# Retention stage of a hybrid decoder layer: bias rows loaded between the token tiles, masked sample values on ScalarE, state products ahead of the samples' output

## The chip, the cores and the metric

The kernel runs on one core of a Trainium2 chip. The metric is the device time of one execution in microseconds (us); less is better. Engine names: PE is TensorE (matmuls and transposes), DVE is VectorE, ACT is ScalarE, POOL is GpSimd, SP is SyncE, which here only issues DMAs. L12 is line 12 of the kernel before.

## The reference, cut to what matters

One decoder layer runs on a prompt (1024 tokens) and on samples (8 sequences of 8 new tokens, so 64 rows). The input projection makes `z`, whose columns are queries, keys, values and gate of the retention and queries, keys, values of the attention. Retention is computed per head (8 heads of width 64) in chunks:

```
inner = einsum('bihd,bjhd->bhij', q, k) * decay
o     = einsum('bhij,bjhe->bihe', inner, v) + einsum('bihd,bhde->bihe', q, S) * cross_decay
S_new = S * exp(C * log_g) + einsum('bjhd,bjhe,jh->bhde', k, v, k_decay)
o     = group_norm(o) * g_ret * silu(gate)
```

The samples bring a state of their own for each sequence (8 x 8 heads x 64 x 64), so their output needs `q @ S` with the old state, and their new state needs `k^T v` within each sequence. The attention, which comes after, adds a bias that depends on the distance of key and query (`rel_bias[t5_bucket(dist)]`); the table of it for the samples, `bias_s`, is built within the retention stage.

## The kernel before, in words

The kernel is a row of stages with a barrier after each: input projection, retention (`retention`, L638), prompt attention, sample attention, output projection and FFN. Only the retention stage is touched. Each engine has its own instruction list there, written out by hand, and the engines meet only through semaphores. The tokens are tiles t = 0 to 7 of 128 prompt rows and tile 8, `SAMPLE`, of 64 sample rows.

**SP (L691 to L715).** In this order: the loads of `zr` tiles 2 to 8 out of scratch memory (L698, issued at L185; tiles 0 and 1 were loaded by the stage before); `tables.load` (L589), which issues `rel_bias` three times into `rel` (L592), the small table `whose` (L593), and the large `dist_s` (L594); after POOL's clearing the state `S_in` (L702); the stores of mix tiles 0 and 1 (`store`, L695); eight loads of the prompt's bias, `bias_p` (L598); the stores of mix tiles 2 to 7; loads for the next stage (L965); the prompt's last state (L712); the store of the samples' mix; a wait until `bias_p` has landed.

**PE (L876 to L957).** For each tile `inner(t+1)` (L896: scores of keys and queries), `output(t)` (L913 and L916), `turn(t+2)` (L885: transposes of q and k), `update(t+1)` (L904: the state). `inner(t)` waits for `inT_ready` t, which DVE's `scores(t-1)` raises. After the loop: the first part of the samples' distance table (`sample_products`, L632, part 0); the samples' output (L938 with the old state, L941 with the inner scores), signalled by `o_done`; the samples' state products (L950), which write the four PSUM banks `su_ps`, `in_ps` (two) and the second of `o_ps`, with one signal for each of the four head pairs; parts 1 and 2 of the table (L632); and, after the samples' output is centred, filler matmuls (`keep_awake`, L146).

**DVE (L770 to L874).** For each tile t: `scores(t)` (L779), `centre(t-1)` (L812, L814, L818), `carry(t+1)` (L799), at t = 2 also `tables.build_rows` (L615: the six products rel times whose), `variance(t-1)` (L824, L826), `finish(t-2)` (L833). `build_rows` waits until all of `rel` and `whose` have landed (`landed` 64). `finish(t)` writes the mix tile into one of two buffers `mixr`, so for t >= 2 it waits until the store of tile t-2 has landed (L832). After the loop: the sample scores, the sample queries (L788), `centre(7)`, `last_state` (L799, L807), `variance(7)`, `finish(6)`, then `one_sequence` for sequences 0 to 4 (L685), `finish(7)`, part 0 of the table out of PSUM (L622), `centre(SAMPLE)`, and four `decode_state` (L866: new state of a head pair) with `variance(SAMPLE)` after the first and `finish(SAMPLE)` after the third.

`vm` holds, for each sequence, the sample values with all other sequences' rows set to zero; `bmask[:, b]` is 1 for the rows of sequence b. DVE makes five of them and POOL three:

```
eng.tensor_tensor(vm[:, b, :], head(SAMPLE, 2, 0, NH).unsqueeze(1).broadcast_to(shape),
                  spread(bmask[:, b], shape), ALU.mult).then_inc(vm_ready, 1)
```

**ACT (L743 to L768).** For each tile `evacuate(t+2)` (L750, L751: q and k out of PSUM) and `square(t)` (L758); at the end `square(SAMPLE)` and parts 1 and 2 of the table (L622).

**POOL (L717 to L741).** For each tile `late(t)` (L728: the power -0.5 of the variance; L730: the product with it), at t = 3 the decayed keys `kd` (L737), at t = 5 its share of `vm` (L685), and at the end `late(SAMPLE)`.

Of the kernel before, what the change touches and what calls it, by code (L numbers as in the profile page):

```python
# [27 lines left out]
ALU = mybir.AluOpType  # L28
# [5 lines left out]
WID = NH * HD  # L34
# [114 lines left out]
def spread(ap, shape):  # L149

    return ap.unsqueeze(2).broadcast_to(shape)
# [9 lines left out]
class RetentionInputs:  # L161
# [21 lines left out]
    def load(self, eng, z, t):  # L183
        n = tile_rows(t)
        eng.dma_start(self.zr[t][0:n].rearrange("p a h d -> p (a h d)"), z[t * 128:t * 128 + n, 0:4 * WID]).then_inc(self.landed[t], 16)  # L185
# [383 lines left out]
class DistanceTables:  # L569
# [16 lines left out]
         self.bias_landed) = map(  # L586
            sem, ("landed", "samples_landed", "ones_set", "rel_t_ready", "bias_done", "bias_ready", "bias_landed"))

    def load(self, sp):  # L589
        sp.wait_ge(self.ones_set, 1)  # L590
        for n in range(3):
            sp.dma_start(self.rel[n * self.K:n * self.K + N_BUCKETS, :], self.A["rel_bias"]).then_inc(self.landed, 16)  # L592
        sp.dma_start(self.whose[:, :], self.A["c_whose"]).then_inc(self.landed, 16)  # L593
        sp.dma_start(self.dist_s[:, :, :], self.A["c_dist_s"]).then_inc(self.samples_landed, 16)  # L594

    def load_bias(self, eng):
# [41 lines left out]
def retention(nc, A, z, mix, ident, ret, state_p, tab, bias_p, bias_s, kept_on, stored, sout_ready, ahead):  # L638


    with ExitStack() as ctx:
# [33 lines left out]
        def head(t, a, h, n=1):  # L675
            return zr[t][0:tile_rows(t), a, h:h + n, :].rearrange("t h d -> t (h d)")

        def by_sequence(p, r):
            return sample_ps[p][HD * r:HD * r + HD].rearrange("d a c -> d (a c)").rearrange("d (b e) -> d b e", e=HD)

        def one_sequence(eng, b):

            shape = [NS, b.stop - b.start, WID]
            eng.wait_ge(landed[SAMPLE], 16)
            eng.tensor_tensor(vm[:, b, :], head(SAMPLE, 2, 0, NH).unsqueeze(1).broadcast_to(shape),  # L685
                              spread(bmask[:, b], shape), ALU.mult).then_inc(vm_ready, 1)

        with nc.Block() as block:

            @block.sync  # L690
            def _(sp):  # L691
                def store(t):
                    rows = tile_rows(t)
                    sp.wait_ge(mix_ready, t + 1)
                    sp.dma_start(mix[t * 128:t * 128 + rows, :], mixr[0:rows, t % 2, :]).then_inc(mix_stored[t % 2], 16)  # L695

                for t in range(2, TT):
                    ret.load(sp, z, t)  # L698
                tables.load(sp)
                sp.wait_ge(cleared, 4)  # L700
                for par in range(2):
                    sp.dma_start(S_in[HD * par:HD * par + HD, :, :, HD * par:HD * par + HD],  # L702
                                 A["state_ret"][0].rearrange("b (p r) d e -> r d b p e", r=2)[par]).then_inc(state_landed, 16)
                store(0)
                store(1)
                tables.load_bias(sp)
                for t in range(2, PT):
                    store(t)
                ahead(sp)
                sp.wait_ge(last_ready, 2)  # L710
                for par in range(2):
                    sp.dma_start(state_p.rearrange("(p r) d e -> r d p e", r=2)[par],  # L712
                                 S_last[HD * par:HD * par + HD]).then_inc(state_stored, 16)
                store(SAMPLE)
                tables.finish(sp)  # L715

            @block.gpsimd  # L717
            def _(pool):
                pool.memset(mhalf[:, :], -0.5).then_inc(cleared, 1)
                pool.memset(S[:, :, :, :], 0.0).then_inc(cleared, 1)  # L720
                pool.memset(qdm[:, :, :], 0.0).then_inc(cleared, 1)
                pool.memset(S_in[:, :, :, :], 0.0).then_inc(cleared, 1)
                pool.wait_ge(cleared, 1)

                def late(t):
                    rows = tile_rows(t)
                    pool.wait_ge(var_ready, t + 1)
                    pool.tensor_tensor(stat[0:rows, t, 4, :], stat[0:rows, t, 3, :], mhalf[0:rows, :], ALU.pow).then_inc(rstd_ready, 1)  # L728
                    pool.wait_ge(rstd_ready, t + 1)
                    pool.tensor_tensor(oc[0:rows, t % 2], oc[0:rows, t % 2], spread(stat[0:rows, t, 4, :], [rows, NH, HD]),  # L730
                                       ALU.mult).then_inc(on_ready, 1)

                for t in range(PT):
                    late(t)
                    if t == 3:
                        pool.wait_ge(landed[SAMPLE], 16)
                        pool.tensor_tensor(kd[:, :, :], zr[SAMPLE][0:NS, 1], spread(last_s[:, :], [NS, NH, HD]),  # L737
                                           ALU.mult).then_inc(kd_ready, 1)
                    if t == 5:
                        one_sequence(pool, slice(DEC_B // 2 + 1, DEC_B))  # L740
                late(SAMPLE)  # L741

            @block.scalar  # L743
            def _(act):
                def evacuate(t):
                    rows = tile_rows(t)
                    act.wait_ge(qk_turned, t + 1)
                    if t >= 2:
                        act.wait_ge(o_done, t - 1)
                    act.copy(qT[:, t % 2, :, 0:rows], qk_ps[0][:, :, 0:rows])  # L750
                    act.copy(kT[:, t % 2, :, 0:rows], qk_ps[1][:, :, 0:rows]).then_inc(qkT_ready, 1)  # L751

                def square(t):
                    rows = tile_rows(t)
                    act.wait_ge(oc_ready, t + 1)
                    if t:
                        act.wait_ge(square_sum_ready, t)
                    act.activation(sq[0:rows], oc[0:rows, t % 2], ACT.Square).then_inc(sq_ready, 1)  # L758

                evacuate(0)  # L760
                evacuate(1)
                for t in range(PT):
                    if t + 2 < TT:
                        evacuate(t + 2)
                    square(t)
                square(SAMPLE)
                for n in (1, 2):
                    tables.build_samples(act, act.copy, n, table_ps[n])  # L768

            @block.vector  # L770
            def _(dve):
# [37 lines left out]
                def centre(t):  # L809
                    rows = tile_rows(t)  # L810
                    dve.wait_ge(o_done, t + 1)
                    dve.tensor_reduce(stat[0:rows, t, 0, :], o_ps[t % 2][0:rows], AXX, ALU.add).then_inc(sum_ready, 1)  # L812
                    dve.wait_ge(sum_ready, t + 1)
                    dve.tensor_scalar(stat[0:rows, t, 1, :], stat[0:rows, t, 0, :], -1.0 / HD, None, ALU.mult).then_inc(mean_ready, 1)  # L814
                    dve.wait_ge(mean_ready, t + 1)
                    if t >= 2:
                        dve.wait_ge(mix_ready, t - 1)
                    dve.tensor_tensor(oc[0:rows, t % 2], o_ps[t % 2][0:rows], spread(stat[0:rows, t, 1, :], [rows, NH, HD]),  # L818
                                      ALU.add).then_inc(oc_ready, 1)
# [33 lines left out]
                last_state()  # L853
                variance(PT - 1)
                finish(PT - 2)
                one_sequence(dve, slice(0, DEC_B // 2 + 1))
                finish(PT - 1)
                tables.build_samples(dve, dve.tensor_copy, 0, table_ps[0])
                centre(SAMPLE)
                dve.wait_ge(state_landed, 32)  # L860

                def decode_state(p):
# [4 lines left out]
                                                 chunk_s[rows, p:p + 1], by_sequence(p, r), ALU.mult, ALU.add).then_inc(sout_ready, 1)  # L867

                decode_state(0)
                variance(SAMPLE)  # L870
                decode_state(1)
                decode_state(2)
                finish(SAMPLE)
                decode_state(3)  # L874

            @block.tensor  # L876
            def _(pe):
# [46 lines left out]
                for t in range(PT):  # L924
# [4 lines left out]
                    if t + 1 < PT:  # L929
                        update(t + 1)  # L930
                tables.sample_products(pe, 0, table_ps[0])
                pe.wait_ge(state_landed, 32)
                pe.wait_ge(qd_ready, 1)
                pe.wait_ge(inT_ready, SAMPLE + 1)
                pe.wait_ge(oc_ready, SAMPLE - 1)
                for p in range(NPAIR):
                    for b in range(DEC_B):
                        pe.matmul(o_ps[0][0:NS, 2 * p:2 * p + 2, :].rearrange("t h d -> t (h d)"),  # L938
# [2 lines left out]
                        mm = pe.matmul(o_ps[0][0:NS, 2 * p + r, :], inT[0:NS, r, p, 0:NS], head(SAMPLE, 2, 2 * p + r),  # L941
                                       start=False, stop=(r == 1))
                mm.then_inc(o_done, 1)
                pe.wait_ge(kd_ready, 1)
                pe.wait_ge(vm_ready, 2)
                pe.wait_ge(last_ready, 2)
                pe.wait_ge(oc_ready, PT)
                for p in range(NPAIR):
                    for r in range(2):
                        mm = pe.matmul(by_sequence(p, r), kd[:, 2 * p + r, :], vm[:, :, HD * (2 * p + r):HD * (2 * p + r + 1)],  # L950
                                       start=True, stop=True)
                    mm.then_inc(update_done, 1)
                pe.wait_ge(qkT_ready, TT)
                for n in (1, 2):
                    tables.sample_products(pe, n, table_ps[n])
# [2021 lines left out]
```

## Time and profile before

| what | us |
|---|---|
| runs of the kernel before (3) | 1560.14 to 1569.92, median 1566.24 |
| profiled execution: time | 1573.37 |
| profiled execution: span | 1571.6 |
| retention stage within the span, first PE instruction to last | 366.06 to 448.43 |
| PE busy over the span | 1489.1 (95%) |
| DVE, ACT, POOL busy | 809.4 (52%), 557.0 (35%), 310.4 (20%) |
| mean granted clock of PE | 0.988 of full speed |

The span is the time from the first to the last record of the profiled execution; the device time has 1.8 us more around it. The profiled execution is 7.1 us longer than the median of the runs. All times in the rows below are us from the start of the span. In a timeline row the first number is the start and the second the time from there to the end of the last of its instructions.

### The profile page before, as it was taken

The numbers are of one execution on the slowest core, as the hardware profiler recorded it, in microseconds if no ns is written. First come the engines' busy times: TensorE is split into PE (matmuls) and PEld (weight loads), VectorE is DVE, ScalarE is ACT, GpSimd is POOL, SyncE is SP. The second block draws the span as 40 slices with busy tenths as digits, with TensorE's granted clock in tenths as the row PEclk, the third lists the DMA queues.
The fourth block names the chain that finished last, engine by engine and source line by source line (L and its number), as shares of the span: only waits on it lengthen the run. The fifth ranks groups of instructions, "written<-read, shape, count | busy, mean of one in ns | idle before, by whom it ended". The sixth has DMA issues, their size and how long they took to land.

```text
span 1571.6 us, 23194 instructions
## 1 busy us (share of the span) xinstructions
PE 1489.1 (95%) x8974; PEld 1279.6 (81%) x8974; DVE 809.4 (52%) x1396; ACT 557.0 (35%) x1054; POOL 310.4 (20%) x362
## 2 busy tenths in 40 slices
PE   7999999998988888898999999999999999999987
PEld 6788888887855556776889999999999999888766
DVE  2333211103766654443456966766676675755455
ACT  4401112212134543443333433343333333545442
POOL 3246420002532323100464010000001000000001
PEclk9999999999899999999999999999999999999999
DMA  5346554527565724993366587989898985877865
GB/s 207 99 134 193 174 188 146 184 97 252 180 222 149 206 78 194 420 408 106 126 197 191 182 210 220 213 225 227 208 237 167 244 194 174 290 241 225 245 232 203
DMA packets 138830, 317.77 MB, mean 202 GB/s; under 512 B 23948, under 2 KB 65180, under 8 KB 133573
## 3 DMA queue, kind: packets, MB, share of 16 engines
q1 hardware_dynamic: 129928, 229.26, 44.0%
q0 software_dynamic: 6976, 71.32, 20.9%
q10 hardware_dynamic: 1824, 15.83, 2.4%
q8 instruction: 65, 1.06, 0.3%
q14 instruction: 37, 0.30, 0.1%
HBM read 254.45 MB, written 137.92 MB: 250 GB/s over the span
## 4 chain that ended last, share of the span: by engine, by line
PE 40%; POOL 3%; DMA 3%; DVE 3%; issue 3%; ACT 1%; SPq 1%; DVEq 0%; POOLq 0%; ACTq 0%
PE y_ps L2760 28%; PE y_ps L2844 4%; PE y_ps L2750 3%; PE x_ps L2844 3%; DMA raw_step<-wt_scratch 2%; POOL xm L1712 1%; POOL h_lo L1726 1%; DVE slot_lo L2447 1%; PE y_ps L1845 1%; DVE y L1810 1%; PE m_ps L2771 1%; PE d_ps L2771 1%; PE m_ps L2844 0%; PE d_ps L2844 0%; SPq L2122 0%
## 5 line engine op out<-in xcount | busy, mean ns | idle before, releaser
L518 PE MATMUL z_ps<-w_hi,h_hi 128*128 128x512 f32 x488 | 191.4, 392 | 4.3 <-POOL h_lo L335 4.3
L518 PE MATMUL z_ps<-w_lo,h_hi 128*128 128x512 f32 x488 | 190.7, 391 | 0.0
L2760 PE MATMUL y_ps<-h_hi,slot_lo 128*128 128x320 f32 (+1 forms) x560 | 179.8, 321 | 0.0
L2760 PE MATMUL y_ps<-h_hi,slot_hi 128*128 128x320 f32 (+1 forms) x560 | 179.8, 321 | 0.0
L2760 PE MATMUL y_ps<-h_lo,slot_hi 128*128 128x320 f32 (+1 forms) x560 | 179.5, 321 | 0.0
L518 PE MATMUL z_ps<-w_hi,h_lo 128*128 128x512 f32 x432 | 168.7, 391 | 0.0
L131 POOL DMA_DIRECT2D ks_sample<-cache_k_win x60 | 34.1, 568 | 630.9 <-PE y_ps L2760 389.4
L2447 DVE TENSOR_TENSOR slot_lo<-raw_step,slot_hi 128x512 fp32r<-128x512 f32 x132 | 85.2, 687 | 85.9 <-ACT slot_hi L2257 85.8
L518 PEld LDWEIGHTS z_ps<-w_hi,h_hi 128*128 128x128 f32 x488 | 91.9, 188 | 24.6 <-POOL h_lo L335 4.9
L2257 ACT CAST slot_hi<-raw_step 128x512 fp32r<-128x512 f32 x132 | 75.3, 618 | 95.0 <-DMA raw_step<-wt_scratch 39.7
L2760 PE MATMUL y_ps<-s_hi,slot_hi 128*128 128x384 f32 x320 | 107.7, 337 | 0.0
L2760 PE MATMUL y_ps<-s_hi,slot_lo 128*128 128x384 f32 x320 | 107.7, 336 | 0.0
L2760 PE MATMUL y_ps<-s_lo,slot_hi 128*128 128x384 f32 x320 | 107.5, 336 | 0.0
L518 PEld LDWEIGHTS z_ps<-w_lo,h_hi 128*128 128x128 f32 x488 | 92.1, 189 | 18.9
L2760 PEld LDWEIGHTS y_ps<-h_hi,slot_lo 128*128 128x128 f32 x560 | 105.2, 188 | 0.0
L2760 PEld LDWEIGHTS y_ps<-h_lo,slot_hi 128*128 128x128 f32 x560 | 105.2, 188 | 0.0
L2760 PEld LDWEIGHTS y_ps<-h_hi,slot_hi 128*128 128x128 f32 x560 | 105.2, 188 | 0.0
L430 DVE TENSOR_TENSOR w_lo<-w_raw,w_hi 128x2048 fp32r<-128x2048 f32 x14 | 32.0, 2288 | 124.1 <-ACT w_hi L365 124.1
L518 PEld LDWEIGHTS z_ps<-w_hi,h_lo 128*128 128x128 f32 x432 | 81.5, 189 | 17.1
L2447 DVE TENSOR_TENSOR slot_lo<-raw,slot_hi 128x512 fp32r<-128x512 f32 x104 | 69.9, 691 | 30.1 <-ACT slot_hi L2257 28.8
L2299 ACT COPY held<-y_ps 128x384 f32<-128x384 f32 x60 | 28.7, 479 | 118.1 <-PE y_ps L2760 118.1
L2257 ACT CAST slot_hi<-raw 128x512 fp32r<-128x512 f32 x104 | 62.2, 619 | 11.3 <-PE y_ps L2760 8.7
(369 smaller groups left out, 3200.7 us busy)
## 6 DMA issues: line engine op xcount, KB each, us to landing
ks_sample<-cache_k_win POOLq DMA_DIRECT2D x60, 544.0 KB, 8.5
vs_sample<-cache_v_win POOLq DMA_DIRECT2D x60, 544.0 KB, 10.9
raw<-w_gu SPq DMA_DIRECT2D x20, 1024.0 KB, 15.4
raw_step<-f_scratch SPq DMA_DIRECT2D x66, 256.0 KB, 3.9
K<-cache_k_win SPq DMA_DIRECT2D x8, 2048.0 KB
w_raw<-w_in SPq DMA_DIRECT2D x14, 1024.0 KB
z_scratch<-z_out SPq DMA_DIRECT2D x56, 256.0 KB, 2.3
raw_d<-w_down SPq DMA_DIRECT2D x11, 1024.0 KB, 12.3
```

Of the source, the lines that this page charges most:

```text
L131: eng.dma_start(flat(new)[:, bass.ds(row * WID, n * WID)], flat(old)[:, bass.ds(row * WID + DEC_T * WID, n * WID)]).then_inc(kept, 16)
L430: dve.tensor_tensor(w_lo[cut], w_raw[:, q], w_hi[cut].bitcast(F32), ALU.subtract).then_inc(w_lo_ready, 1)
L518: mm = pe.matmul(z_ps[t % 3][:, :], x[:, k, t * 128:t * 128 + 128], w[:, par, k, :], start=(k, n) == first, stop=(k, n) == last)
L1712: pool.tensor_tensor(self.xm[:, t % 2, :], self.y[:, :], self.inputs.x_n[:, t % 2, :], ALU.add).then_inc(self.xm_ready, 1)
L1726: pool.tensor_tensor(self.h.lo[at][cut], self.hg[:, q, :, 0:n], self.h.hi[at][cut].bitcast(F32), ALU.subtract).then_inc(self.lo_ready, 1)
L2257: act.copy(in_slot(slot_hi, n), source(n)).then_inc(hi_ready, 1)
L2299: act.copy(held[:, k, :], chain_a[:, 0:384]).then_inc(held_ready, 1)
L2447: dve.tensor_tensor(in_slot(slot_lo, n), source(n), in_slot(slot_hi, n).bitcast(F32), ALU.subtract).then_inc(lo_ready, 1)
L2750: mm = pe.matmul(bank[u % 2][:, 0:n], w, x, start=(k, m) == (0, 0), stop=(k, m) == (KT - 1, 2))
L2760: mm = pe.matmul(bank[:, 0:cols], w, v[:, k, :], start=fresh and (k, m) == (0, 0), stop=(k, m) == (HK - 1, 2), skip_group_check=True)
L2771: mm = pe.matmul(sample_ps[c], f_s[:, sub, :], w[n % RING][:, :], start=(g, sub, e) == (0, 0, 0), stop=(g, sub, e) == (LAST, 1, 1), skip_g ...
L2844: mm = pe.matmul(bank, x[:, own], w[:, :], start=fresh and m == 0, stop=ends and m == 2, skip_group_check=True)
```

## The change

Four edits, all in the retention stage.

1. `tables.load` is split. The three loads of `rel` and the one of `whose` are issued after the `zr` loads of tiles 2 and 3; `dist_s` keeps its place behind all seven.
2. DVE's five masked sample values go to ACT, as five copies with a scale of one column of `bmask`: two after `square(6)`, three after `square(7)`. POOL keeps its three. `vm_ready` thus reaches 6 instead of 2.
3. Part 0 of the table goes out of PSUM on ACT, after those three copies, in place of DVE.
4. PE issues the samples' state products before the samples' output. DVE does all four `decode_state` first, then `centre`, `variance` and `finish` of the samples.

```diff
-    def load(self, sp):
+    def load_rows(self, sp):
         sp.wait_ge(self.ones_set, 1)
         for n in range(3):
             sp.dma_start(self.rel[...], self.A["rel_bias"]).then_inc(self.landed, 16)
         sp.dma_start(self.whose[:, :], self.A["c_whose"]).then_inc(self.landed, 16)
+
+    def load_distances(self, sp):
         sp.dma_start(self.dist_s[:, :, :], self.A["c_dist_s"]).then_inc(self.samples_landed, 16)
...
+        ON_ACT = DEC_B // 2 + 1
...
                 for t in range(2, TT):
                     ret.load(sp, z, t)
-                tables.load(sp)
+                    if t == 3:
+                        tables.load_rows(sp)
+                tables.load_distances(sp)
...
+                def own_values(sequences):
+                    act.wait_ge(landed[SAMPLE], 16)
+                    for b in sequences:
+                        act.activation(vm[:, b, :], head(SAMPLE, 2, 0, NH), ACT.Copy, scale=bmask[:, b:b + 1]).then_inc(vm_ready, 1)
...
                     square(t)
+                    if t == 6:
+                        own_values(range(2))
+                own_values(range(2, ON_ACT))
+                tables.build_samples(act, act.copy, 0, table_ps[0])
                 square(SAMPLE)
...
                 finish(PT - 2)
-                one_sequence(dve, slice(0, DEC_B // 2 + 1))
                 finish(PT - 1)
-                tables.build_samples(dve, dve.tensor_copy, 0, table_ps[0])
-                centre(SAMPLE)
                 dve.wait_ge(state_landed, 32)
...
                 decode_state(0)
-                variance(SAMPLE)
                 decode_state(1)
                 decode_state(2)
+                decode_state(3)
+                centre(SAMPLE)
+                variance(SAMPLE)
                 finish(SAMPLE)
-                decode_state(3)
...
                 tables.sample_products(pe, 0, table_ps[0])
+                pe.wait_ge(kd_ready, 1)
+                pe.wait_ge(vm_ready, 1 + ON_ACT)
+                pe.wait_ge(last_ready, 2)
+                pe.wait_ge(oc_ready, PT)
+                pe.wait_ge(inT_ready, SAMPLE + 1)
+                for p in range(NPAIR):
+                    for r in range(2):
+                        mm = pe.matmul(by_sequence(p, r), kd[...], vm[...], start=True, stop=True)
+                    mm.then_inc(update_done, 1)
                 pe.wait_ge(state_landed, 32)
                 pe.wait_ge(qd_ready, 1)
-                pe.wait_ge(inT_ready, SAMPLE + 1)
-                pe.wait_ge(oc_ready, SAMPLE - 1)
                 for p in range(NPAIR):
...
                 mm.then_inc(o_done, 1)
-                pe.wait_ge(kd_ready, 1)
-                pe.wait_ge(vm_ready, 2)
-                pe.wait_ge(last_ready, 2)
-                pe.wait_ge(oc_ready, PT)
-                for p in range(NPAIR):
-                    for r in range(2):
-                        mm = pe.matmul(by_sequence(p, r), kd[...], vm[...], start=True, stop=True)
-                    mm.then_inc(update_done, 1)
                 pe.wait_ge(qkT_ready, TT)
```

## Rows read from the trace of the kernel before

**Rows 1.** Waits of all engines, 362 to 450 us: total us, times, longest.

```profile
DVE rel_t L615 <- DMA whose<-c_whose: 6.9, 1, 6.9
```

**Rows 2.** Timeline of DVE in the tile loop: start, us, and idle before it in brackets.

```profile
391.29 0.63 DVE L615 TENSOR_TENSOR rel_t<-rel,whose 99x24 f32<-99x24 f32 x6 [6.86 <-DMA whose<-c_whose]
...
402.28 1.29 DVE L779 TENSOR_TENSOR inT<-in_ps,mask 128x512 f32<-128x512 f32 x2 [3.31 <-PE o_ps L916]
...
406.69 0.69 DVE L833 TENSOR_TENSOR mixr<-oc,zr 128x512 f32<-128x512 f32 x1
...
421.19 1.29 DVE L779 TENSOR_TENSOR inT<-in_ps,mask 128x512 f32<-128x512 f32 x2 [0.93 <-PE o_ps L916]
...
423.11 2.50 DVE L814 TENSOR_SCALAR stat<-stat 128x8 f32<-128x8 f32 x1
```

**Rows 3.** Timeline of PE in the tile loop.

```profile
394.78 2.08 PE L896 MATMUL in_ps<-qT,kT 64*128 64x128 f32 x16 [6.23 <-DVE inT L779]
...
405.04 1.16 PE L896 MATMUL in_ps<-qT,kT 64*128 64x128 f32 x16 [0.26 <-ACT kT L751]
...
411.07 1.16 PE L896 MATMUL in_ps<-qT,kT 64*128 64x128 f32 x16 [0.27 <-ACT kT L751]
```

**Rows 4.** Busy us of PE, PEld, DVE, ACT, POOL; PEclk; DMA share; GB/s.

```profile
396.00:400.00 4.00, 4.00 (x24) 3.78 (x22) 2.89 (x6) 0.63 (x1) 1.55 (x1) 0.50 0.70 156
```

**Rows 5.** Landing: zr tiles 2 and 3; stores 0 and 1; the eight bias_p loads.

```profile
DMA to landing us min/median/max: 5.2/6.2/7.3
...
DMA to landing us min/median/max: 3.4/4.1/4.8
...
DMA to landing us min/median/max: 4.9/7.2/9.8
```

**Rows 6.** DMA issues between 407.3 and 407.9 us: KB, us to landing (mix store 2).

```profile
mix_scratch<-mixr SPq DMA_DIRECT2D x1, 256.0 KB, 7.0
```

**Rows 7.** Timeline of SP's issues.

```profile
373.07 24.09 SPq L702 DMA_DIRECT2D S_in<-state_ret  x1
397.20 2.14 SPq L695 DMA_DIRECT2D mix_scratch<-mixr  x2
399.39 4.97 SPq L598 DMA_DIRECT2D bias_p<-tab_scratch  x8
```

**Rows 8.** Timeline of PE at the end of the stage.

```profile
429.47 1.93 PE L938 MATMUL o_ps<-S_in,qdm 128*64 128x128 f32 x16 [0.60 <-DVE qdm L788]
...
438.34 0.22 PE L941 MATMUL o_ps<-zr,inT 64*64 64x64 f32 x1
...
440.92 1.08 PE L950 MATMUL o_ps<-vm,kd 64*64 64x512 f32 x4
...
446.55 1.88 PE L146 MATMUL o_ps<-zr,ident 128*128 128x512 f32 x4
```

**Rows 9.** Timelines of ACT, DVE and POOL.

```profile
361.88 0.72 ACT L392 ACTIVATE z_out<-sums,stat 64x512 f32<-64x512 f32 x1 [0.76 <-DVE sums L436]
...
430.94 0.63 ACT L758 ACTIVATE sq<-oc 128x512 f32<-128x512 f32 x1 [3.95 <-DVE oc L818]
...
437.76 0.69 DVE L833 TENSOR_TENSOR mixr<-oc,zr 128x512 f32<-128x512 f32 x1 [0.94 <-POOL oc L730]
...
446.89 1.52 DVE L866 SCALAR_TENSOR_TENSOR S_out<-S_in,chunk_s,o_ps 64x512 f32<-64x512 f32 x2
...
443.11 1.63 POOL L728 TENSOR_TENSOR stat<-stat,mhalf 64x8 f32<-64x8 f32 x1 [5.38 <-DVE stat L826]
```

**Rows 10.** Timeline of PE: two long idles in the FFN stage.

```profile
1474.47 0.50 PE L2844 MATMUL y_ps<-slot_hi,slot_hi 128*128 128x512 f32 x1 [3.58 <-DVE slot_lo L2447]
...
1504.31 0.50 PE L2844 MATMUL x_ps<-slot_hi,slot_hi 128*128 128x512 f32 x1 [3.22 <-DVE slot_lo L2447]
```

**Rows 11.** Busy time by stretch behind these two idles; columns as in rows 4.

```profile
1475.80:1479.20 3.40, 3.40 (x10) 2.63 (x9) 3.40 (x6) 2.59 (x6) 0.00 (x0) 0.53 0.93 341
...
1504.30:1508.00 3.70, 3.04 (x12) 2.17 (x12) 3.70 (x7) 2.95 (x7) 0.00 (x0) 1.00 0.29 111
```

More of the change, by code:

```diff
@@ L679, in by_sequence @@
             return sample_ps[p][HD * r:HD * r + HD].rearrange("d a c -> d (a c)").rearrange("d (b e) -> d b e", e=HD)
[L681 to L686, printed above, removed]
+        ON_ACT = DEC_B // 2 + 1
         with nc.Block() as block:
@@ L739, in _ @@
                     if t == 5:
-                        one_sequence(pool, slice(DEC_B // 2 + 1, DEC_B))
+                        shape = [NS, DEC_B - ON_ACT, WID]
+                        pool.tensor_tensor(vm[:, ON_ACT:, :], head(SAMPLE, 2, 0, NH).unsqueeze(1).broadcast_to(shape),
+                                           spread(bmask[:, ON_ACT:], shape), ALU.mult).then_inc(vm_ready, 1)
                 late(SAMPLE)
@@ L931, in _ @@
                 tables.sample_products(pe, 0, table_ps[0])
+                pe.wait_ge(kd_ready, 1)
[5 more added lines that the diff above has]
+                    for r in range(2):
+                        mm = pe.matmul(by_sequence(p, r), kd[:, 2 * p + r, :], vm[:, :, HD * (2 * p + r):HD * (2 * p + r + 1)],
+                                       start=True, stop=True)
+                    mm.then_inc(update_done, 1)
                 pe.wait_ge(state_landed, 32)
                 pe.wait_ge(qd_ready, 1)
-                pe.wait_ge(inT_ready, SAMPLE + 1)
-                pe.wait_ge(oc_ready, SAMPLE - 1)
                 for p in range(NPAIR):
@@ L943, in _ @@
                 mm.then_inc(o_done, 1)
-                pe.wait_ge(kd_ready, 1)
-                pe.wait_ge(vm_ready, 2)
-                pe.wait_ge(last_ready, 2)
-                pe.wait_ge(oc_ready, PT)
-                for p in range(NPAIR):
-                    for r in range(2):
-                        mm = pe.matmul(by_sequence(p, r), kd[:, 2 * p + r, :], vm[:, :, HD * (2 * p + r):HD * (2 * p + r + 1)],
-                                       start=True, stop=True)
-                    mm.then_inc(update_done, 1)
                 pe.wait_ge(qkT_ready, TT)
```

## The prediction

> **What bounds the kernel now.** I read the page first: PE is busy 95% of the span, so only time that PE loses in this stage, or adds to its end, can count. The waits of the stage have one row that does not repeat with the tiles: DVE stands 6.9 us before the six small products of `build_rows` [rows 1]. The timelines show what hangs on it. DVE is free at 391.29 - 6.86 = 384.4 and starts at 391.3 [rows 2]; `scores(3)` is queued behind it, and PE idles 6.23 us for it before `inner(4)` [rows 3]. Then comes a second loss: with the granted clock at 0.50, the lower of the two levels (1.2 GHz), from just before PE restarts [rows 4], the tile that starts at 394.78 lasts 10.26 us, where the next lasts 6.03 [rows 3]. So this one wait costs 6.23 - 0.27 = 6.0 us idle and 4.2 us of slow work, 10.2 us together. At the end of the stage PE runs from the samples' output through the state products and the tables to the filler, 429.5 to 448.43, with no gap worth naming [rows 8], and DVE ends at 446.89 + 1.52 = 448.41 [rows 9]: the two are balanced there.
>
> **Edit 1, rows behind tiles 2 and 3.** Tiles 2 and 3 land 5.2 and 7.3 us after their issue at about 366.0 and 366.5, so by 374 [rows 5]. The four small loads (3 x 1.0 KB, 1.2 KB) stand right behind; even several us late they beat 384.4. No load is added, and the tiles behind move by the issue time of four small loads at most, some 2 us, while tile 5's transposes come only near 393. So the 6.9 us wait goes. Bounds: nothing (if the rows still land last) and the whole 10.2 us.
>
> What is late next is SP's queue. SP is held in the second `S_in` issue until 373.07 + 24.09 = 397.16 and only then issues store 0, at 397.20 [rows 7], landing 4.8 us later, at 402.0 (store 1 at 402.4) [rows 5]. Nothing in the change moves this. Before, `finish(2)`, which needs that store landed, came at 406.69 [rows 2] and never met it. With 10.2 us taken out its iteration would start at 392.9 (one tile pitch and the 6.0 us, 402.28 - 9.4: `scores(4)` had also stood behind the slow matmuls) and `finish(2)` would come 4.4 us later, at 397.3. It must wait until 402.0 and ends at 402.7; behind it on DVE is `scores(5)`, 402.7 to 404.0, for which PE's `inner(6)` waits. `inner(6)` starts at 404.1 instead of 411.07 [rows 3]: the gain is 7.0 us, not 10.2, and PE idles about 3.5 us.
>
> There is a second such place. Store 2 stands behind the eight loads of `bias_p`, whose issue ends at 404.36 [rows 7], the last landing at 403.9 + 9.8 = 413.7 [rows 5]; before, it was issued at 407.4 and landed 7.0 us later, 414.4 [rows 6]. It will land at the same time, since the 4 MB ahead of it do. `finish(4)` then is due at 412.6 and starts at 414.4; `scores(7)` starts at 415.1 instead of 421.19 [rows 2]: the gain is 6.1 us. Against that, L814 took 2.50 us at 423.11 [rows 2] beside POOL's share of `vm`; in the new phase they overlap by 1.6 us or so: 0.8 us back for DVE's chain. **Head: 6.9 us gained.**
>
> **Edits 2 to 4, the end, in the times of before.** ACT has no copy of this form in this stage; the nearest rows are the scaled copy of 64x512, 0.72 us [rows 9], and, from below, no time at all for what ACT's idle hides (two of the five fall before `square(7)`, 4 us of idle [rows 9]). I take 0.6 us for each of the three that count, between the pitch of back-to-back copies and 0.72. They follow `square(7)`, which ends at 430.94 + 0.63 = 431.57, so `vm` is ready at 433.4 (bounds 431.6 and 433.8). PE now waits for that before it may do anything of the samples: its product of part 0 ended 0.60 us before 429.47 [rows 8], so it idles some 4.6 us, or 3.8 after the head's unequal shifts. Behind this wait stand output, state products and both table parts.
>
> - State products 433.5 to 437.2 (before 438.3 to 442.0, 3.7 us [rows 8]).
> - Output, 429.47 to 438.56 before, 9.1 us [rows 8]: ends at 446.3.
> - PE then: tables 4.7 us (442.0 to 446.6 before) and filler 1.9 [rows 8]: 452.9.
> - Beside it the samples' norm: centre 1.6, square 0.65, variance 0.9, POOL 2.8 (L728 1.63 [rows 9] and the product), `finish` 0.7, SP's store 0.5: 7.1 us, so 453.4.
>
> The stage ends at 453.4 against 448.4: **the end costs 5.0 us.** What the edits save on DVE is true but hidden: the masked values and part 0 leave it, `finish(7)` comes no later than 437.76 [rows 9], and four `decode_state` of 1.52 us [rows 9] end by 438.5 + 6.1 = 444.6, before the output they used to stand beside. The old order had PE work on the output while `vm` was made; the new one leaves that cover unused.
>
> **The clock.** Two new idles, 3.5 and 3.8 us, can throw PE to its lower level. Of two like idles in the trace, 3.58 us was followed by a stretch at 0.53 and 3.22 us by none [rows 10, 11]; the 6.2 us one cost 4.2 us [rows 3, 4]. A stretch like 1475.8 to 1479.2 costs half its length, 1.7 us. Bounds for each place: 0 and 4.2 us. I take one short stretch at each: 1.7 at the end, and in the loop 0.8, because 0.9 us of it lies in the second store's wait. By the Trainium skill (TensorE: Matmul & The Clock Gate, What's actually happening) the throttled state is the default and activity releases it, which speaks against an order that opens idle on PE; the 3.22 us idle without a fall shows that here it is a matter of chance as well.
>
> **Sum.** -6.9 + 5.0 + 0.8 + 1.7 = +0.6 us on a profiled execution of 1573.37 us: 1574.0. That execution lay 7.1 us above the median, 1566.24, so the median after is 1566.8 us. A measurement of this kernel tells about 1% (16 us) from no change, and its own three runs span 10 us. The forecast is no measurable change.
>
> **The rivals.**
> - **A, the whole head is won.** `finish(2)` and `finish(4)` do not wait, and the clock stays up. For it: PE keeps a 6.03 us pitch wherever it is fed [rows 3]. Against it: the issue at 397.20 and its landing. It gives -(10.2 + 0.8) + 5.0 = -6.0: 1560.2 us. Chance 0.15.
> - **B, slower by the clock.** The mechanism is the half-speed stretch behind the new waits at `finish(2)` and ahead of the state products, each as long as the one of before: 4.2 at the end and 3.3 in the loop, so -6.9 + 5.0 + 7.5 = +5.6: 1571.8 us. It decides once the slow stretches cost more than the 1.9 us that the rest gains. This is what the page's rule makes of two idles. For it: that stretch has small matmuls like the ones here [rows 3]. Against: the one of 3.4 us [rows 11]. Chance 0.25.
> - **C, the rows do not land earlier.** The small loads complete only with what follows; the head is unchanged and the end costs 5.0 + 1.7: 1572.9 us. For it: `whose` landed only after all that was issued before it. Against: tiles 2 and 3 landed early [rows 5]. Chance 0.05.
>
> **How the numbers follow.** The forecast holds 0.55, with a range of its own of 1563 to 1570. Adding A, B and C and the spread of the runs, 1559 to 1573 holds 8 in 10. Only several errors in one direction pass 1%: faster 0.02, within 1% 0.95, slower 0.03.
>
> **What would show it.** L615 without an idle before it, near 384.4. `mixr` L833 of tile 2 waiting for the landing of a store, near 402, and again near 414; PE idle 3 to 4 us before `inner(6)`. At the end PE idle about 4 us before the first L950, released by ACT `vm`; L938 behind L950; the stage ending 1 to 2 us earlier than 448.4 where the clock stays up, later where it does not. Wrong would be: stores landing well before 400, `vm` ready before 431 in the times of before, or a stage end moved by over 6 us either way.

## The result, and the profile after

The kernel after takes 1575.44 us in the median of 14 runs (1568.34 to 1583.90), the kernel before, run beside it, 1565.83 us (14 runs, 1560.14 to 1569.92). The ratio is 1.0062, 95% interval 1.0045 to 1.0080: slower by 9.6 us, 0.6%. The prediction was no measurable change, 1566.8 us in a range of 1559 to 1573. So the forecast of "within 1%" held, but the time lies outside the range, and the loss is clear of the runs' noise. Of the runs used below, two of the kernel before (1583.36 and 4353.76 us) and one of j1 (4554.69 us) were slow runs and are left out of the medians.

The profiled execution of the kernel after took 1572.07 us (span 1570.2). From the stage's first PE instruction to the next stage's first it has 88.7 us (362.69 to 451.39), the kernel before 83.4 us (366.06 to 449.50). That is 5.3 us more, of the 9.6 of the medians. One chance thing is in it: the clock was at its lower level for 3.4 us at the very start of the stage of the kernel after (364.6 to 368.2), so its first state update began 5.75 us into the stage against 4.25 before, 1.5 us lost ahead of anything that was changed.

The waits of all engines of the kernel after, 362 to 450 us (total us, times, longest), no longer have the row of [rows 1]; the forecast wait for the stores stands among them:

```profile
DVE mixr L843 <- DMA mix_scratch<-mixr: 4.5, 2, 2.3
```

The timeline of DVE of the kernel after (start, us, idle before in brackets):

```profile
382.60 0.64 DVE L617 TENSOR_TENSOR rel_t<-rel,whose 99x24 f32<-99x24 f32 x6
...
397.74 1.19 DVE L843 TENSOR_TENSOR mixr<-oc,zr 128x512 f32<-128x512 f32 x1 [2.20 <-DMA mix_scratch<-mixr]
...
411.38 1.11 DVE L843 TENSOR_TENSOR mixr<-oc,zr 128x512 f32<-128x512 f32 x1 [2.27 <-DMA mix_scratch<-mixr]
...
442.71 0.68 DVE L822 TENSOR_REDUCE stat<-o_ps 64x8 f32<-64x512 f32 x1 [8.54 <-PE o_ps L957]
```

`build_rows` starts at once, where it had 6.86 us of idle before it [rows 2]; `finish(2)` and `finish(4)` wait for stores 0 and 2. At the end DVE is idle for 8.5 us until the samples' output is done, and its last `finish` ends at 449.4. The timelines say why, of PE:

```profile
400.39 1.16 PE L904 MATMUL in_ps<-qT,kT 64*128 64x128 f32 x16 [1.66 <-DVE inT L789]
...
413.96 0.68 PE L904 MATMUL in_ps<-qT,kT 64*64 64x64 f32 x16 [1.83 <-DVE inT L789]
...
418.50 5.43 PE L634 MATMUL table_ps<-dist_s,rel_t 99*128 99x512 f32 x6
424.01 1.97 PE L947 MATMUL su_ps<-vm,kd 64*64 64x512 f32 x4
425.75 3.65 PE L947 MATMUL in_ps<-vm,kd 64*64 64x512 f32 x8
429.16 1.94 PE L947 MATMUL o_ps<-vm,kd 64*64 64x512 f32 x4
431.03 3.67 PE L954 MATMUL o_ps<-S_in,qdm 128*64 128x128 f32 x16
```

and, of ACT,

```profile
421.99 1.93 ACT L764 ACTIVATE vm<-zr,bmask 64x512 f32<-64x512 f32 x3
```

The three late copies take 1.93 us, 0.64 each (forecast 0.6), and PE's first state product starts at their end, 423.9. The 4 us of idle that were forecast there are not in this profile: part 0 of the table, at half clock, ended at the same moment, 423.9, and hid the wait. Everything of PE from 416 to 436 runs slowly: part 0 of the table 5.43 us where it was 2.8 before, state products 424.0 to 431.1 (7.1 us against 3.7), output 431.0 to 442.6 (11.6 against 9.1 [rows 8]). Busy time by stretch (columns as in rows 4):

```profile
411.00:416.00 5.00, 3.17 (x38) 2.94 (x37) 4.37 (x6) 0.76 (x3) 4.09 (x2) 1.00 0.14 54
416.00:424.00 8.00, 7.93 (x20) 4.31 (x19) 6.43 (x16) 4.23 (x8) 3.07 (x2) 0.50 0.09 33
424.00:431.00 7.00, 6.99 (x16) 1.86 (x16) 4.22 (x6) 0.56 (x1) 3.06 (x2) 0.50 0.40 125
431.00:436.00 5.00, 5.00 (x26) 4.52 (x25) 3.04 (x5) 0.00 (x0) 0.00 (x0) 0.50 0.64 169
436.00:443.00 7.00, 7.00 (x59) 6.18 (x58) 0.29 (x1) 0.00 (x0) 0.00 (x0) 0.97 0.00 0
```

For 20 us PE is busy almost without a gap, at a granted clock of 0.50 (the 1.2 GHz level), from 416.0 to 436.4. It fell 2.0 us after PE had restarted from the 1.83 us idle before 413.96; that this idle caused it is the likely reading, not a shown one. The state products and the output alone lose 3.4 + 2.5 = 5.9 us.

All runs together say the same. Every run lists PE's mean granted clock; (1 - clock) x time is an estimate of what the lower level costs it. Its mean is 25.1 us over the 14 runs of the kernel after and 16.4 us over 102 runs of the kernel before that were taken beside the experiments below (no clocks are on record for the 14 of the result). The difference, 8.7 us, is nearly the whole of the loss; what is left of the time, 1550.5 and 1549.7 us, is the same within 1 us. So outside the clock the head's gain and the new wait cancel, much as the prediction had it. (The clock is listed to 0.001, which is 1.6 us in one run.)

### The profile page after: what moved, and what is told of

Same layout as the page of the kernel before. It is cut to its first block, busy times and chain, and to the rows that moved or that the text cites. A ratio compares the mean times of both kernels' runs of the same rounds, so it can differ in the third digit from the quotient of the medians.

```text
span 1570.2 us, 23197 instructions
## 1 busy us (share of the span) xinstructions
PE 1493.1 (95%) x8974; PEld 1279.9 (82%) x8974; DVE 805.4 (51%) x1394; ACT 561.0 (36%) x1060; POOL 310.0 (20%) x362
## 4 chain that ended last, share of the span: by engine, by line
PE 41%; POOL 3%; DMA 3%; DVE 3%; issue 2%; ACT 1%; SPq 0%; DVEq 0%; POOLq 0%; ACTq 0%
PE y_ps L2767 28%; PE y_ps L2851 4%; PE y_ps L2757 3%; PE x_ps L2851 3%; DMA raw_step<-wt_scratch 2%; POOL xm L1719 1%; POOL h_lo L1733 1%; PE y_ps L1852 1%; DVE slot_lo L2454 1%; DMA x_m<-x_mid_scratch 1%; DVE y L1817 1%; PE m_ps L2778 1%; PE d_ps L2778 1%; PE m_ps L2851 1%; PE d_ps L2851 1%
```

## The experiments

Medians are of runs beside the kernel before on the same chip, whose median was 1565.0 to 1566.8 us throughout; ratios are against it. The e, g, j, k and l runs were each taken on another chip, so a difference between groups is given by its ratios too where they say something else. "Stage" is the length as above, from the one profile, and "end" its part from tile 8's inner product on. "Clock" is the mean over the runs of the estimate (1 - clock) x time.

| kernel | median us | ratio (95%) | stage us | end us | clock us |
|---|---|---|---|---|---|
| before (beside e) | 1565.0 | | 83.4 | 26.8 | 15.0 |
| after | 1575.44 | 1.0062 (1.0045 to 1.0080) | 88.7 | 37.4 | 25.1 |
| e1 edit 1 alone | 1566.22 | 1.0002 (0.9985 to 1.0019) | 77.3 | 26.1 | 16.7 |
| e2 edits 2 to 4 | 1580.79 | 1.0096 (1.0074 to 1.0118) | 94.3 | 37.6 | 24.2 |
| e3 edits 1 to 3 | 1566.70 | 1.0008 (0.9991 to 1.0026) | 79.8 | 26.1 | 17.4 |
| e4 after + filler | 1570.07 | 1.0037 (1.0018 to 1.0057) | 80.8 | 31.5 | 17.4 |
| g1 e3, states cut | 1562.09 | 0.9967 (0.9942 to 0.9991) | 74.8 | 26.9 | 14.7 |
| g2 after, states cut | 1571.40 | 1.0024 (1.0010 to 1.0038) | 87.6 | 36.4 | 21.7 |
| j1 g2 + filler | 1566.45 | 1.0009 (0.9990 to 1.0027) | 80.2 | 32.2 | 14.5 |
| j2 e3, stores first | 1557.72 | 0.9949 (0.9929 to 0.9969) | 73.5 | 27.0 | 12.2 |
| j3 edit 1, stores first | 1559.10 | 0.9954 (0.9933 to 0.9976) | 73.5 | 27.0 | 13.8 |
| k3 e1 + 5 fillers in the loop | 1565.18 | 0.9995 (0.9981 to 1.0010) | 78.8 | 26.8 | 14.5 |
| l1 e1 + 3 fillers in the loop | 1566.61 | 0.9993 (0.9970 to 1.0016) | 77.9 | 26.1 | 14.9 |

The stages of e4, j1 and k3 hold a slow 3.4 us at their start, as that of the kernel after does (1.5 us of the stage's length).

**The edits apart.** e1 is the kernel before with edit 1; e2 the changed kernel without it; e3 has PE's and DVE's order of before back:

```diff
-                (state products, with their waits)
                 (output of the samples)
+                (state products, with their waits)
                 pe.wait_ge(qkT_ready, TT)
```

> The kernel before with edit 1 alone. Both theories of the loss (order: the state products wait ahead of the samples' output; clock: the new wait lets PE's clock fall and it stays low through what follows) put it in the end of the stage, which is not touched here: the head's 6.9 us less 0.8 for the clock, so 6 us below the kernel before, some 1560 us. Rival: the waits for the stores, which this edit uncovers, give it back: within 2 us of the kernel before, or above it.

> The changed kernel with edit 1 undone (edits 2 to 4 alone). Order theory: 5.0 us and at most one short slow stretch of 1.7: 5 to 7 us above the kernel before, some 1572 us. Clock theory: the slow stretch covers state products and output, 3 + 2.5 us and more: 10 to 12 us above, some 1577 us. If the end costs as much as in the changed kernel while the head loses its gain, it must lie above the changed kernel.

> The changed kernel with edit 4 undone: edits 1 to 3, but state products behind the output as before, and DVE's order as before. If the order (with or without the clock) is the loss, it is as fast as edit 1 alone or 1 us faster, some 1559 us. Rival: the copies on ACT are the loss, and it stays near the changed kernel, 1573 us or more.

e3 is the verdict on edits 2 and 3: with them and the old order the time is that of e1, to some 3 us. The loss is edit 4: e3 to the kernel after is 1566.7 to 1575.4. Edits 2 to 4 without edit 1 (e2) cost 15.0 us by the ratio. That is above even what the clock theory had (10 to 12); the expectation's 1559 us for e3 was missed as well, since it counted on e1's gain. By the estimate from the clock, 9.3 us of e2's loss against the kernel before beside it are the clock, and 5.6 us are the rest. In e2 PE idled for the masked values and all behind it ran slowly, by the timeline of PE and then the busy time by stretch (columns as in rows 4) of e2:

```profile
433.52 1.97 PE L943 MATMUL su_ps<-vm,kd 64*64 64x512 f32 x4 [4.63 <-ACT vm L760]
```

```profile
433.00:445.00 12.00, 11.47 (x38) 5.92 (x39) 7.74 (x12) 0.89 (x2) 3.06 (x2) 0.51 0.49 143
```

The idle of 4.63 us is the 4.6 us of the prediction; the slow stretch, 13.7 us long, is what was not in the sum. e1 missed: edit 1 alone gives nothing, where 6 us were forecast; its rival, that the waits for the stores give the gain back, has the time.

**The clock at the end.** e4 puts matmuls on PE ahead of the waits for the state products:

```diff
                 tables.sample_products(pe, 0, table_ps[0])
+                pe.wait_ge(oc_ready, SAMPLE - 1)
+                keep_awake(pe, o_ps[0][:, :, :], ident[:, :], head(2, 0, 0, NH), 4)
                 pe.wait_ge(kd_ready, 1)
```

> The changed kernel with four filler matmuls of 128x128 by 512 columns (1.9 us at full clock, 3.4 at the lower) on PE ahead of the wait for the masked values. Order theory: PE waits there anyway and the clock matters little, so no change against the changed kernel, 0 to +2 us. Clock theory: the filler lifts the clock or keeps it up, state products (7.0 us against 3.7) and output (11.6 against 9.1) shorten, 3 to 6 us below the changed kernel, some 1570 us.

The timeline of PE, and then the busy time by stretch, of e4:

```profile
418.12 3.60 PE L146 MATMUL o_ps<-zr,ident 128*128 128x512 f32 x8
422.22 1.08 PE L949 MATMUL su_ps<-vm,kd 64*64 64x512 f32 x4 [0.50 <-ACT vm L764]
```

```profile
418.00:436.00 18.00, 17.50 (x108) 11.33 (x107) 12.23 (x23) 2.94 (x5) 4.82 (x4) 1.00 0.37 110
```

The fillers took 3.60 us, not the 1.9 of the expectation (four fillers are eight matmuls in the trace). The time fell by 5.4 us against the kernel after (3.9 by the ratios, whose intervals overlap) although PE had more to do, and the clock's share fell from 25.1 to 17.4 us. In this profile the clock had not fallen in the loop either, so one thing was still open: whether the fall comes from the loop's waits or from the new one. g2 takes the second of the loop's two waits away and leaves 1.75 us of PE's idle at the first, j1 adds the fillers again, and g1 is g2 with the old order:

```diff
-                (S_in of all eight sequences)
+                load_states(slice(0, DEC_B // 2))
                 store(0)
                 store(1)
+                load_states(slice(DEC_B // 2, DEC_B))
+                store(2)
                 tables.load_bias(sp)
```

> Edits 1 to 3 with the order of before (as e3), and the loads of the samples' states cut in two halves: one ahead of mix stores 0 and 1, one behind them, and the bias loads behind store 2. If the waits for the stores (3.2 us in e3) and the slow stretch behind them (10.2 us long in e3) eat the head's gain, both go: the inner product of tile 8 starts near 50 us after the stage's start instead of 53.6, and the median lies 4 to 6 us below e3, some 1561 us. Rival: the head's time is hidden or given back later, within 2 us of e3.

> The changed kernel with the same cut of the state loads. If the slow stretch at the end starts from the loop's waits (1.7 and 1.8 us idle), it goes with them: PE then waits 3 to 5 us for the masked values at full clock, and the median falls to some 1567 us. Rival: the wait for the masked values alone makes the clock fall, as in e2 (4.6 us idle, 13.7 us slow): the loop gains 3 us, state products and output stay slow, some 1572 us.

> g2 with the four fillers of e4 ahead of the wait for the masked values. Clock theory: the fillers keep the clock up at the end of the stage, state products take 3.7 us instead of 7.0 and the output 9.1 instead of 10.4 or more; 4 to 5 us below g2, some 1567 us, and what is left against g1 (1562 us), which has the order of before, is the wait itself, 4 to 5 us. Rival: the fillers helped e4 by chance (its clock did not fall in the loop either), no change against g2, 1571 us.

g1 and j1 came where they were forecast. g2 came at its rival's 1572 us: it keeps the slow end. By its timeline PE idled 3.83 us ahead of the state products and then took 1.89 us for the first four of them; with the fillers (j1, second fence) they take 1.08 us.

```profile
427.24 1.89 PE L952 MATMUL su_ps<-vm,kd 64*64 64x512 f32 x4 [3.83 <-ACT vm L769]
```

```profile
423.37 1.08 PE L954 MATMUL su_ps<-vm,kd 64*64 64x512 f32 x4 [1.20 <-ACT vm L769]
```

In g2's profile the clock had fallen in the loop too, for 6.8 us, but was back at full level from 411 on and fell anew at this wait, for 10.2 us. So the clock can be lost at the wait for the masked values too, with the level full before it; how much the loop's idle adds in the kernel after is not shown. With one SP order, the new PE order costs 1571.4 - 1562.1 = 9.3 us, on one chip. The fillers bring back 4.9 of it by the medians (j1, another chip) and 2.3 by the ratios, and lower the clock's share from 21.7 to 14.5 us, that of g1. What remains is the wait: 4.4 us by the medians, 6.6 by the ratios, and in the profiles, where the end ran at full level, 32.2 - 26.9 = 5.3 us (e4 against before: 31.5 - 26.8 = 4.7). The prediction had 5.0.

**The head.** Why edit 1 alone gives nothing. j2 and j3 put mix stores 0 and 1 ahead of both halves of the state loads (j2 on e3, j3 on e1):

```diff
-                load_states(slice(0, DEC_B // 2))
                 store(0)
                 store(1)
+                load_states(slice(0, DEC_B // 2))
+                store(2)
                 load_states(slice(DEC_B // 2, DEC_B))
-                store(2)
```

> g1 with mix stores 0 and 1 ahead of both halves of the state loads. The 1.7 us idle that g1 keeps before the inner product of tile 6 waits for store 0, which stands behind the first half: it goes, and the inner product of tile 8 starts near 46.5 us after the stage's start (g1: 47.9). Median 1 to 3 us below g1, some 1560 us. Rival: SP, held by the issue of the state loads later now, delays store 2 or the bias loads, and the time stays or rises by 2 us.

> The kernel before with edit 1 and the SP order of j2, and nothing of edits 2 to 4. If edits 2 and 3 only take hidden work off DVE, it is within 1 us of j2; if DVE becomes the bound of the end of the stage once the head is short, it is 1 to 3 us above j2.

In e1 `finish(2)` waited for store 0; the same line of j2 does not (timelines of DVE, e1 and then j2):

```profile
400.99 0.69 DVE L837 TENSOR_TENSOR mixr<-oc,zr 128x512 f32<-128x512 f32 x1 [3.76 <-DMA mix_scratch<-mixr]
```

```profile
397.14 0.69 DVE L848 TENSOR_TENSOR mixr<-oc,zr 128x512 f32<-128x512 f32 x1
```

j3 against e1 is -7.1 us: the head's gain is real, and the stores behind the state loads had held it. In the profiles the stage falls from 83.2 (mean of three of before) to 73.5 us, 9.7 of the 10.2 that rival A gave to the whole head. j2 went beyond its forecast (1 to 3 us below g1): 4.4. j2 is 1.4 us faster still than j3, inside the spread of the runs; edits 2 and 3 show no worth by themselves. j2 is also the version that beats both kernels, by 8.5 us and 17.7 us.

The rest of the head went to one question: is it the store's wait or the clock falling behind it?

```diff
                 for t in range(PT):
+                    if t == 5:
+                        keep_awake(pe, tables.ps[:, :], ident[:, :], head(2, 0, 0, NH), 5)
                     inner(t + 1)
```

> Edit 1 alone (e1), with five filler matmuls of 128x128 by 512 columns (2.3 us at full clock) on PE ahead of the inner product of tile 6, where PE idles 2.7 us for the stores. If the clock falling there is what takes back the head's gain in most runs, it goes: 3 to 5 us below e1, some 1562 us. Rival: the waits for the stores alone take it back, no change against e1, 1566 us.

> k3 with three fillers in place of five. k3's five took 4.5 us (each is two matmuls, 0.9 us), 1.8 us more than the idle there, and gave back what the clock won (its clock lost 3 us less than e1's). Three take 2.7 us, which is e1's idle. Clock theory: 2 to 4 us below e1 (1566.2), some 1563 us. Rival: again 1565 us or more, and the clock in the loop is worth nothing by itself.

Both misses for the clock theory. In l1's profile the fillers filled most of the idle and the clock stayed at full level through the whole stage, even past an idle of 1.83 us like that of the kernel after (timeline of PE). Yet the median is e1's:

```profile
400.33 2.74 PE L146 MATMUL table_ps<-zr,ident 128*128 128x512 f32 x6
404.14 1.16 PE L900 MATMUL in_ps<-qT,kT 64*128 64x128 f32 x16 [1.07 <-DVE inT L783]
...
417.71 0.68 PE L900 MATMUL in_ps<-qT,kT 64*64 64x64 f32 x16 [1.83 <-DVE inT L783]
```

The clock's share did fall, from 16.7 us (e1) to 14.5 and 14.9, but the rest of the time rose as much. So in the loop it is the wait for the stores; a gain of the time from the clock alone is not shown there, and one of up to 4 us in k3 is not excluded by the spread of the runs.

Last, profiles of kernels already run, to see how far one profile can be trusted. The kernel before:

> The kernel before once more, for a second profile. Edit 1 took 6.1 us out of the stage's profile but nothing out of the medians. If the profiled execution of before is typical, the stage is again 83 us long with a slow stretch of some 10 us behind the 6.2 us idle. Rival: that stretch is a matter of chance; here it is 3 to 7 us long, and the stage 80 to 82 us.

> A third profile of the kernel before, same question: stage length 83 us again, or shorter with a shorter slow stretch or a shorter wait for the rows.

Edit 1 alone:

> Edit 1 alone once more, for a second profile. e1's profile had a slow stretch of 3.4 us in the loop and a stage of 77.3 us, yet its median equals that of the kernel before. If the profile of e1 was a lucky one, the slow stretch is 7 to 14 us long here (as in e3, which has the same loop) and the stage 79 to 82 us.

> A third profile of edit 1 alone, same question: stage of 77 us again, or 79 to 82 us with a longer slow stretch.

The stage of before was 82.7 and 83.5 us, as in the first profile (83.4), each with a 10.2 us slow stretch behind the wait for the rows. Edit 1 alone had 80.9 and 79.4 us after 77.3: the first was the luckiest, the clock having fallen for 3.4 us in it and for 10.2 in the other two. On average 83.2 and 79.2, so 4 us of e1's gain are in the profiles and still not in the medians. A hint: the three profiled executions of before had mean clocks of 0.988, 0.986 and 0.989 where the median of its runs is 0.990, so the stall may cost less in an ordinary execution than in a profiled one. Against it: e2 has the head of before, with the same 10.2 us stretch, and its profiled execution (1580.71 us) is at its median (1580.79). This stays open.

## Why the prediction was wrong, point by point

- **What bounds, the wait for the rows, the two waits for the stores:** right. L615 had no idle; the stores' waits came in the same two places. In the profile they cost PE 1.7 and 1.8 us instead of 3.5 and 0.9. For the first, store 0 was issued 30.3 us after the stage's start against 31.1 before, and DVE came to `finish(2)` 32.9 us after it, not 31.2, most of that by the slow start of the stage. The loop's gain up to tile 8's inner product is 5.4 us, or 6.9 without that start (forecast 6.1).
- **Head: 6.9 us gained.** Right in the profile, too much in the medians when edit 1 stands alone: there it gives 0 (e1). It is worth 5.4 us when the end is the changed one (e2 to after, 1580.8 to 1575.4), and 7.1 us once the stores no longer wait (e1 to j3). The sum took the parts as independent; the medians give edit 1 another worth beside each end and each SP order, with some 3 us of spread on each.
- **The end costs 5.0 us:** right for the wait itself: 4.7 and 5.3 us in the profiles with the clock kept up, 4.4 (medians) or 6.6 (ratios) in j1 against g1.
- **Masked values at 0.6 us each on ACT, nothing saved by unloading DVE:** right, 0.64 us, and e3 equals e1.
- **The clock, "one short stretch at each: 1.7 at the end":** this is the step that failed. For the end with its clock the sum had 5.0 + 1.7 = 6.7 us; e2 measures 15.0, and that difference, 8.3 us, is nearly all of the 9.0 by which +0.6 missed +9.6. The slow stretch at the end lasted 20.5 us in the kernel after, 13.7 in e2 and 10.2 in g2. In the kernel after it cost 5.9 us in state products and output by the profile; over all runs the clock's share rose by 8.7 us (after) and 9.3 us (e2), by the estimate. I had bounded it at 4.2 us by the stretch in the loop, and took 1.7 from one in the FFN stage [rows 11]. Nothing in the sum allowed for a stretch longer than any in the trace. What ends such a stretch these runs do not settle. Rival B had the mechanism and a chance of 0.25, but at 4.2 us in place of 5.9 and more its 1571.8 us is still 3.6 too low.
- **The level the sum was set against.** 1573.37 us less 7.1 for the median took the whole profile as one long sample. All three profiles of before have the 10.2 us stretch, and the head's gain was counted on to remove it; whether ordinary executions lose as much there is not shown. It cannot have made the miss of the end, since e2 keeps that stretch.

The Trainium skill (TensorE: Matmul & The Clock Gate, What's actually happening) says that the throttled state is the default and that activity releases it. The traces agree in part: the falls in e2 and g2 came with idles of 4.63 and 3.83 us, but idles of 1.66 us (kernel after, before 400.39) and 1.83 us (l1) brought none. That work brings the level back the kernel after shows only late: PE stayed at 0.50 for 20 us while it was busy 7.93 of 8.00 us, 6.99 of 7.00 and 5.00 of 5.00 in the stretches above, and came back at 436.4, amid the output's matmuls.

## What to carry to other kernels

An instruction order that makes PE wait, with the long work behind the wait, costs the wait, and it may cost half the speed of all that stands behind it besides: price the slow stretch up to the whole of that work, not by the shortest stretch in the trace. Fillers in the idle are a cheap test, and half a cure; keeping an independent piece of work for that place, as the old order did, is the cure. When a wait in a loop is taken out, look first at what SP's queue can deliver earlier: here 7 us lay behind loads that nobody needed yet.

## What the runs showed that was not expected

PE's clock can stay at its lower level under unbroken work: 416.0 to 436.4 us in the kernel after. Before, the same part 0 of the table and the same products ran at full level; the clock had not fallen there. And about half of the spread from run to run of one kernel goes with the clock: in the kernel after, 1568.3 us at a mean clock of 0.988 and 1583.9 us at 0.979.
